# Flow turns of two attention stages: where mask tables are made, when finished chunks are copied out, and how next-turn projection work is spread

## The chip, the cores and the metric

One Trainium2 chip, one core. The program is one launch. The metric is device microseconds of that core, from three runs of the kernel before: 3243.58, 3242.65 and 3238.93, median 3242.65.

The engines are named as the profile names them: PE (TensorE), ACT (ScalarE), DVE (VectorE), POOL (GpSimd) and SP (SyncE, here only a DMA queue).

## The reference, cut to what matters

The model is two blocks in a row. The change touches two of their mixers. Each has 16 heads of width 64, over 1024 tokens. The first is forgetting attention (`fox` in the kernel):

```python
logits = einsum('bhtd,bhsd->bhts', qb, kb) * d ** -0.5 + F[:, :, q0:q1, None] - F[:, :, None, :q1]
probs  = softmax(where(mask_causal, logits, -inf)); out = probs @ vb      # F = cumsum(log_sigmoid(fz + fb))
y_f    = out * silu(fg)
```

The second is neighbourhood attention on a 16 x 64 grid with 256 context tokens (`nb` in the kernel):

```python
s   = einsum(q_r, k_reg) * d ** -0.5 + bias(rel_bias);  s = where(col_mask, s, NEG_INF)
p   = softmax(concatenate([s, q_r @ kc]));  o = p_lat @ v_reg + p_ctx @ vc
y   = (o * silu(g)) @ w_out
```

In both, q, k, v and g are projections of the same activations with a 1024-row weight matrix.

## The kernel before, in words

**Turns.** Both mixers are run by the class `Flow`. It works on two heads at a time, so each mixer has 8 turns (`PAIRS`). `plan` writes out by hand, before the program is built, one list of steps for each turn. PE, ACT and DVE each walk the same list and do their own part of each step, in its order, and wait on semaphores for each other. So the list is the order of each engine's queue.

**Fill.** The projections of float32 values are done as three matmuls (high x high, low x high, high x low). One chunk of a projection (512 tokens, or 256 for the context) takes 24 matmuls (`FULL`). Step `F n` issues the next n of them. Turn `it` fills with V and G of its own heads and with Q and K of the next turn's heads. That is 8 chunks in a fox turn (192 matmuls) and 10 in an nb turn (240). Chunks alternate between two PSUM banks, and step `E` copies a finished chunk out: for Q and K, ACT writes the high part and DVE then the low part. The first score of a turn (`head` in `pe`) waits for the last chunk of the turn before.

**Attention.** `S` is a score piece: PE multiplies, then DVE (line 1455) subtracts it from a mask table, writes it to SBUF and keeps the running minimum. There is one pair of score banks, so each `S` on PE waits until DVE has finished the one before. `X` is the exponential on ACT. A group `T` transposes up to four 128 x 128 blocks, ACT casts them to the high part, DVE subtracts for the low part (line 1466), and one group later `V` multiplies them with the values. There are two transpose banks, so `T` of group n waits until DVE has finished group n-2, counted over all groups. A fox turn has 20 groups in four segments, an nb turn has 26. The scores of segment s+1 are issued among the groups of segment s. `M`, `O`, `N` move, add and normalise a finished segment, `I` inverts its row sums.

**The end of a turn.** After the last group come the remaining `M`, `O`, `N` with 4 fill matmuls ahead of each, then `W` (ACT: silu of the gate), `Y` (DVE multiplies by the gate, line 1504; then ACT makes the high part, line 1416), the rest of the chunk, `D` (DVE subtracts for the low part, line 1509; ACT issues the two stores), and then the mask tables `B` for the next turn. A turn has two of these. In fox they are `nf_tri` for each head (line 1614). In nb they are `nb_bias` (line 2450) and `nb_mid` (line 2453), each for both heads. `L` is their load: ACT waits until all scores of the turn are shifted, then issues two DMAs. In the kernel before, `L` stands after the last group.

**Weights.** SP loads a 128 x 1024 unit of weights, and POOL splits it in two parts with two instructions (lines 210 and 212) as soon as PE has used up the unit that held the slot.

In fox the units' chunks are tokens 0 to 511, then 512 to 1023. The segments of query blocks go (4, 5), (6, 7), (2, 3), (0, 1).

Where the steps stand, counted in fill matmuls of a turn, in the kernel before. Fox: scores of the first segment at 6, 14, 23 and 31; groups from 57 to 144; last five `N`, `I`, `M`, `O`, `N` at 148 to 164; `D` and first table at 168; second table at 192. Nb: scores of the first segment at 6, 20, 35 and 49; groups from 81 to 168; last `N` at 180; `D` and first table at 192, second table at 216; end at 240.

Of the kernel before, what the change touches and what calls it, by code (L numbers as in the profile page):

```python
# [55 lines left out]
def build_program(nc, a):  # L56
# [9 lines left out]
    with ctx:  # L66
# [925 lines left out]
        class Flow:  # L992
# [109 lines left out]

            def plan(self, before, turns, final, tables, last_fill, side_by_side=False):

# [8 lines left out]
                def chunks_of(units, scores_before, side_by_side=False):  # L1113
                    new = []
                    parts = [(unit, i) for unit in units for i in range(len(unit[3]))]
                    if side_by_side:
                        parts.sort(key=lambda part: part[1] >= 2)
                    for (kind, it, unit, spans), i in parts:
                        c0, n = spans[i]
                        last, seq = i == len(spans) - 1, len(self.chunks)  # L1120
                        beside = side_by_side and seq < 4
                        b = (self.p_bank, self.p_bank + 1, self.o_bank, self.o_bank + 1)[seq] if beside \
                            else self.p_bank + seq % 2
                        count[final[kind]] += 1
                        count["chunk"] += not last
                        ch = {"kind": kind, "it": it, "unit": unit, "c0": c0, "n": n, "first": i == 0,
                              "last": last, "seq": seq, "scored": scores_before, "bank": b, "beside": beside,
                              "waits": self.user.get(b),
                              "done": (w_used, unit + 1) if last else (self.chunk, count["chunk"]),
                              "out": ({"act": self.act_out, "dve": self.dve_out}[final[kind]], count[final[kind]])}  # L1130
                        self.user[b] = ch["out"]
                        self.chunks.append(ch)
                        new.append(ch)
                    return new
# [9 lines left out]
                self.seg0 = count["seg"]  # L1144
                self.lead, l_turned = [], [0, 0]
                first = chunks_of(before, count["S"], side_by_side)
# [7 lines left out]
                for it, units in enumerate(turns):  # L1154
                    fill = chunks_of(units, count["S"] + n_scores)
                    steps, held = [], []
                    at = {"fill": 0, "S": 0}

                    scores, base_u = [], count["U"]
# [11 lines left out]
                    def fill_to(n):  # L1171
                        n = min(n, FULL * len(fill))
                        while at["fill"] < n:
# [3 lines left out]
                            if at["fill"] % FULL == 0:  # L1177
                                ch = fill[at["fill"] // FULL - 1]
                                if ch["kind"] in "QK" and at["S"] < n_scores:
                                    held.append(ch)  # L1180
                                else:
                                    steps.append(("E", ch))

                    def score(s):
                        s["l_free"] = l_turned[s["seg"] % 2]
                        steps.append(("S", s))
                        at["S"] += 1
                        if at["S"] == n_scores:
                            steps.extend(("E", ch) for ch in held)

# [7 lines left out]
                    lead = FULL * len(values)  # L1198
                    places = [(6 + (lead - 14) * i // len(scores[0]), "S", s) for i, s in enumerate(scores[0])]
                    places += [(FULL * (i + 1) + 9, "T", ch) for i, ch in enumerate(values)]  # L1200
# [11 lines left out]
                    n_groups = sum(len(g) for g in groups)  # L1212
                    start, main = at["fill"], FULL * sum(ch["kind"] in "VGQ" for ch in fill)
                    if final_turn:
                        n_groups = last_fill
                    todo, waiting, done = [], None, 0

                    def event():
# [5 lines left out]
                    for seg, rows in enumerate(groups):  # L1224
                        count["seg"] += 1
                        pending = list(scores[seg + 1]) if seg + 1 < len(scores) else []
                        for i, (items, adds) in enumerate(rows):
                            g = group("P", it, seg=seg, seg_n=count["seg"], items=items, adds=adds, starts=i == 0,
                                      ends=i == len(rows) - 1, exped=base_u + self.first_unit(seg + 1))
# [31 lines left out]
                    if final_turn:  # L1261
# [5 lines left out]
                        break  # L1267
                    steps.append(("L", it + 1, count["S"]))
                    while todo:
# [4 lines left out]
                    steps.append(("D", it, self.whole))  # L1274
                    for part in range(tables):
                        steps.append(("B", it + 1, part))
# [268 lines left out]
        def fox_units(it, kinds):  # L1545
            return [(kind, it, U_FOX + 4 * it + "QKVG".index(kind), [(0, CH), (CH, CH)]) for kind in kinds]

# [845 lines left out]
        def nb_units(it, kinds):  # L2393
# [5 lines left out]
                {"Q": "dve", "K": "dve", "V": "act", "G": "act"}, 2,  # L2399
                sum(len(nb.seg_groups(seg)) for seg in range(2)), True)  # L2400

# [299 lines left out]
```

## Time and profile before

| | |
|---|---|
| Median of three runs | 3242.65 us |
| Span of the profiled execution, first to last instruction | 3236.3 us |
| PE busy | 96% of the span |
| DVE busy | 62% |
| ACT busy | 40% |
| POOL busy | 23% |
| One fox turn (turns 1 to 6) | 77.03 us |
| One nb turn (turns 1 to 6) | 95.53 us |

The span is the time from the first to the last instruction of one execution. The 8 fox turns run from about 598 to 1215 us, the 8 nb turns from about 2363 to 3100 us. The last turn of each mixer has no next turn to fill with, and has its own layout. Matmul ends are modelled, so the idle time shown ahead of a matmul can be smaller than the time that was lost: start times are the safer reading.

### The profile page before, as it was taken

To read this page: it belongs to the slowest core of one execution; us is meant where nothing else is said; L and a number is where in the kernel's file an instruction comes from. 1 tells how busy PE (TensorE), PEld (TensorE's weight loads), DVE (VectorE), ACT (ScalarE), POOL (GpSimd) and SP (SyncE) were. 2 spreads that over 40 slices of the span, in tenths; PEclk is the share of its full clock that TensorE was granted. 3 is DMA by queue.
4 is the path that set the end of the run, shared out by engine and by line. 5 is a ranking of instruction groups with operands and counts; after the bars stand their busy time and mean duration, and the time that the engine had idled before them with its cause. 6 is when DMAs were issued, how large, how long until landed. Compare 5 with 4: busy or idle time off the path is not lost.

```text
span 3236.3 us, 47842 instructions
## 1 busy us (share of the span) xinstructions
PE 3109.7 (96%) x18134; PEld 2578.9 (80%) x18134; DVE 1999.7 (62%) x3834; ACT 1299.9 (40%) x2340; POOL 759.8 (23%) x324
## 2 busy tenths in 40 slices
PE   9999999999999989999899999999899999999987
PEld 6888888777777767877799889888677778777765
DVE  5676677555565657975755555556755555655555
ACT  5534443444444440022444444440344444454412
POOL 3223332322222213543211121113112112111221
PEclk9999999999999999999999999999999999999999
DMA  3111111111111137521200010153201111100141
GB/s 118 46 40 46 46 59 46 60 59 53 53 53 53 64 146 298 220 79 52 91 30 30 31 43 30 46 203 130 78 21 51 45 51 45 51 32 33 67 161 76
DMA packets 64828, 237.79 MB, mean 73 GB/s; under 512 B 7008, under 2 KB 10080, under 8 KB 63600
## 3 DMA queue, kind: packets, MB, share of 16 engines
q1 hardware_dynamic: 31680, 115.91, 9.9%
q10 hardware_dynamic: 32944, 119.10, 9.7%
q8 instruction: 135, 2.21, 0.3%
q14 instruction: 69, 0.57, 0.0%
HBM read 185.11 MB, written 49.87 MB: 73 GB/s over the span
## 4 chain that ended last, share of the span: by engine, by line
PE 79%; DVE 9%; ACT 5%; issue 2%; DVEq 2%; DMA 1%; ACTq 1%; SPq 0%
PE ps L1304 21%; PE ps L189 13%; PE ps L360 9%; PE ps L2223 7%; PE ps L1368 5%; PE ps L1334 4%; PE ps L1350 4%; PE ps L891 3%; PE ps L482 3%; PE ps L868 2%; PE ps L133 2%; DVE fox_l L1455 1%; PE ps L852 1%; DVE wa_l L941 1%; PE ps L853 1%
## 5 line engine op out<-in xcount | busy, mean ns | idle before, releaser
L210 POOL TENSOR_TENSOR w_hi<-raw,small 128x1024 fp32r<-128x1024 f32 x160 | 334.9, 2093 | 2393.7 <-PE ps L1304 1099.3
L212 POOL TENSOR_TENSOR w_lo<-raw,w_hi 128x1024 fp32r<-128x1024 f32 x160 | 424.8, 2655 | 22.8
L1304 PE MATMUL ps<-nb_u_hi,w_hi 128*128 128x512 f32 (+1 forms) x640 | 249.2, 389 | 6.1 <-DVE nb_q_lo L2470 4.2
L1304 PE MATMUL ps<-nb_u_hi,w_lo 128*128 128x512 f32 (+1 forms) x640 | 246.6, 385 | 0.0
L1304 PE MATMUL ps<-nb_u_lo,w_hi 128*128 128x512 f32 (+1 forms) x640 | 245.7, 384 | 0.0
L1466 DVE TENSOR_TENSOR nb_pt_lo<-ps,nb_pt_hi 128x512 fp32r<-128x512 f32 x208 | 143.9, 692 | 144.2 <-ACT nb_pt_hi L1393 143.9
L360 PE MATMUL ps<-u_hi,w_hi 128*128 128x512 f32 x528 | 212.8, 403 | 5.9 <-ACT silu_h L539 2.6
L1304 PE MATMUL ps<-u_hi,w_lo 128*128 128x512 f32 x512 | 208.9, 408 | 0.0
L360 PE MATMUL ps<-u_hi,w_lo 128*128 128x512 f32 x528 | 208.6, 395 | 0.0
L360 PE MATMUL ps<-u_lo,w_hi 128*128 128x512 f32 x528 | 208.4, 395 | 0.0
L1304 PE MATMUL ps<-u_hi,w_hi 128*128 128x512 f32 x512 | 208.3, 407 | 0.0
L1304 PE MATMUL ps<-u_lo,w_hi 128*128 128x512 f32 x512 | 207.5, 405 | 0.0
L1393 ACT CAST nb_pt_hi<-ps 128x512 fp32r<-128x512 f32 x208 | 122.1, 587 | 193.4 <-PE ps L1350 190.7
L1466 DVE TENSOR_TENSOR fox_pt_lo<-ps,fox_pt_hi 128x512 fp32r<-128x512 f32 (+1 forms) x160 | 102.0, 638 | 129.3 <-ACT fox_pt_hi L1393 128.8
L2223 PE MATMUL ps<-wa_u_hi,w_hi 128*128 128x512 f32 (+1 forms) x480 | 173.1, 361 | 4.3 <-DVE wa_u_lo L2156 1.9
L891 PE MATMUL ps<-wa_v,wa_pt 128*128 128x64 f32 x1344 | 176.5, 266 | 0.0
L2223 PE MATMUL ps<-wa_u_lo,w_hi 128*128 128x512 f32 (+1 forms) x480 | 171.1, 356 | 0.0
L2223 PE MATMUL ps<-wa_u_hi,w_lo 128*128 128x512 f32 (+1 forms) x480 | 171.0, 356 | 0.0
L902 ACT ACTIVATE wa_l<-wa_l,wa_nm 128x641 f32<-128x641 f32 (+2 forms) x160 | 119.3, 746 | 124.8 <-DVE wa_nm L941 123.6
L891 PEld LDWEIGHTS ps<-wa_v,wa_pt 128*128 128x128 f32 x1344 | 168.9, 192 | 0.0
L1393 ACT CAST fox_pt_hi<-ps 128x512 fp32r<-128x512 f32 (+1 forms) x160 | 87.0, 544 | 144.8 <-PE ps L1350 144.3
L1304 PEld LDWEIGHTS ps<-nb_u_hi,w_hi 128*128 128x128 f32 x640 | 121.6, 190 | 29.3 <-issue 11.6
(357 smaller groups left out, 8027.8 us busy)
## 6 DMA issues: line engine op xcount, KB each, us to landing
raw<-in_w_stream SPq DMA_DIRECT2D x160, 512.0 KB, 3.3
h_sb<-in_w_ada ACTq DMA_DIRECT2D x16, 1024.0 KB, 5.0
nf_b<-nf_rows ACTq DMA_DIRECT2D x16, 512.0 KB, 4.4
nb_bias<-in_rel_bias ACTq DMA_DIRECT2D x16, 448.0 KB, 3.8
y_parts<-wa_y_hi ACTq DMA_DIRECT2D x8, 640.0 KB, 3.0
y_parts<-wa_y_lo ACTq DMA_DIRECT2D x8, 640.0 KB, 4.2
la_out_yh<-y_parts SPq DMA_DIRECT2D x8, 640.0 KB, 10.0
la_out_yl<-y_parts SPq DMA_DIRECT2D x8, 640.0 KB, 11.1
```

The costliest lines, as they stand in the source:

```text
L189: mm = pe.matmul(out, w(slot, tiles[i]), u[:, first + i, cols], start=start and i == 0 and p == 0, stop=stop and i == len(tiles) - 1 and p ...
L210: pool.tensor_tensor(w_hi[:, s, :], raw[:, s, :], zero, ALU.add)
L212: pool.tensor_tensor(w_lo[:, s, :], raw[:, s, :], w_hi[:, s, :].bitcast(F32), ALU.subtract).then_inc(w_ready, 1)
L360: mm = pe.matmul(ps[:, b:b + CH], w(slot, k), u[:, k, ch["c"] * CH:(ch["c"] + 1) * CH], start=k == 0 and p == 0, stop=k == KT - 1 and p == 2)
L891: mm = pe.matmul(ps[:, o0:o0 + HD], self.pt[0:n, self.v_place[g] % 3, (c - c0) * P:(c - c0 + 1) * P], vals[0:n, vb, cols], start=c == 0, s ...
L1304: mm = pe.matmul(ps[:, b:b + ch["n"]], w(slot, k), u[:, k, ch["c0"]:ch["c0"] + ch["n"]], start=k == 0 and p == 0, stop=k == KT - 1 and p == 2)
L1334: mm = pe.matmul(ps[:, o:o + n], q[r, qc], k[r, key:key + n], start=p == 0, stop=p == 2)
L1350: mm = pe.transpose(out[:, j * P:(j + 1) * P], self.l_of(g["seg"], qi, hd)[:, l0:l0 + P], ident)
L1368: mm = pe.matmul(ps[:, o + o0:o + o0 + n], self.v[:, vb, kv if self.shared else hd, :], pt[:, g["high"] % 2, p0:p0 + n], start=g["starts"] ...
L1393: nc.scalar.copy(self.pt_hi[:, g["high"] % 2, 0:w], ps[:, t:t + w]).then_inc(self.high, 1)
L1466: dve.tensor_tensor(self.pt_lo[:, i, 0:w], ps[:, t:t + w], self.pt_hi[:, i, 0:w].bitcast(F32), ALU.subtract).then_inc(self.freed, 1)
L2223: mm = pe.matmul(ps[:, b * CH + t:b * CH + t + n], w(i % 2, k), u[:, k, t:t + n], start=k == 0 and p == 0, stop=k == KT - 1 and p == 2)
```

## The change

Five things in `Flow.plan`, and one in each mixer's call.

1. `pieces_until` counts, for each Q and K chunk, after how many score pieces of a turn its columns are no longer needed. A finished chunk is held back only for those, no longer for all scores.
2. In fox, the chunks of Q and K are made in the order tokens 512 to 1023, then 0 to 511.
3. `main`, the fill that is spread over the groups, has one K chunk more: 6 chunks become 7 in fox, 7 become 8 in nb. So 24 fill matmuls move from behind the last group to among the groups.
4. `L` is issued one group after the last score, and from three groups later one `B` is put ahead of each group. What isn't made there stays behind `D`.
5. The scores of the first segment are placed by their size, and in nb (`ahead_by` 1) the first piece of the second segment comes ahead of the groups as well.

In the last turn of a mixer 3 and 4 do nothing.

```diff
+            def pieces_until(self, kind, c0, n):
+                last, at = 0, 0
+                for blk in (blk for blocks in self.segments for blk in blocks):
+                    for piece in blk["pieces"]:
+                        at += 1
+                        spans = [(blk["b"] * P, P)] if kind == "Q" else [(key, w) for _, key, w in piece["runs"]]
+                        if any(a < c0 + n and c0 < a + w for a, w in spans):
+                            last = at
+                return last
...
+                        after = self.pieces_until(kind, c0, n) if kind in "QK" and self.turns is not None else 0
-                              "last": last, "seq": seq, "scored": scores_before, "bank": b, "beside": beside,
+                              "last": last, "seq": seq, "scored": scores_before + after, "after": after,
+                              "bank": b, "beside": beside,
...
-                    fill = chunks_of(units, count["S"] + n_scores)
+                    fill = chunks_of(units, count["S"])
+                    all_scored = count["S"] + n_scores
...
-                                if ch["kind"] in "QK" and at["S"] < n_scores:
+                                if at["S"] < ch["after"] or held:
                                     held.append(ch)
...
-                        if at["S"] == n_scores:
-                            steps.extend(("E", ch) for ch in held)
+                        while held and held[0]["after"] <= at["S"]:
+                            steps.append(("E", held.pop(0)))
...
-                    places = [(6 + (lead - 14) * i // len(scores[0]), "S", s) for i, s in enumerate(scores[0])]
+                    ahead = scores[0] + scores[1][:ahead_by]
+                    sizes = [sum(n for _, _, n in s["blk"]["pieces"][s["piece"]]["runs"]) + 3 * P // 2 for s in ahead]
+                    places = [(6 + (lead - 14) * sum(sizes[:i]) // sum(sizes), "S", s) for i, s in enumerate(ahead)]
...
-                    start, main = at["fill"], FULL * sum(ch["kind"] in "VGQ" for ch in fill)
+                    first_k = [ch for ch in fill if ch["kind"] == "K"][:1]
+                    start, main = at["fill"], FULL * (sum(ch["kind"] in "VGQ" for ch in fill) + len(first_k))
...
+                    since, made = -1 if final_turn else 0, 0
...
+                            since += since > 0 or since == 0 and at["S"] == n_scores
+                            if since == 1:
+                                steps.append(("L", it + 1, all_scored))
+                            if since > 3 and made < tables:
+                                steps.append(("B", it + 1, made))
+                                made += 1
...
-                    steps.append(("L", it + 1, count["S"]))
...
-                    for part in range(tables):
+                    for part in range(made, tables):
...
         def fox_units(it, kinds):
-            return [(kind, it, U_FOX + 4 * it + "QKVG".index(kind), [(0, CH), (CH, CH)]) for kind in kinds]
+            return [(kind, it, U_FOX + 4 * it + "QKVG".index(kind), [(CH, CH), (0, CH)] if kind in "QK"
+                     else [(0, CH), (CH, CH)]) for kind in kinds]
...
-                sum(len(nb.seg_groups(seg)) for seg in range(2)), True)
+                sum(len(nb.seg_groups(seg)) for seg in range(2)), True, 1)
```

## Rows read from the trace of the kernel before

**Rows 1.** The page, first part: busy time of each engine, its share and instructions.
```profile
PE 3109.7 (96%) x18134; PEld 2578.9 (80%) x18134; DVE 1999.7 (62%) x3834; ACT 1299.9 (40%) x2340; POOL 759.8 (23%) x324
```
**Rows 2.** Windows, a fox and an nb turn: length, busy (instructions), PE clock, DMA.
```profile
745.27:822.30 77.03, 75.32 (x434) 59.21 (x433) 45.91 (x122) 35.86 (x74) 17.95 (x9) 1.00 0.15 55
2523.33:2618.86 95.53, 93.53 (x595) 75.19 (x595) 54.28 (x125) 44.87 (x83) 17.15 (x9) 1.00 0.12 43
```
**Rows 3.** PE's waits in that fox turn: total us, times, longest.
```profile
PE ps L1334 <- DVE fox_nm L1455: 0.9, 3, 0.4
PE ps L1350 <- DVE fox_pt_lo L1466: 0.6, 1, 0.6
```
**Rows 4.** PE's waits in that nb turn, same columns.
```profile
PE ps L1350 <- ACT nb_l L1384: 1.4, 2, 0.8
PE ps L1334 <- DVE nb_nm L1455: 0.5, 1, 0.5
```
**Rows 5.** Timeline of PE at a fox turn's end: start, length, line, out<-in [idle before].
```profile
748.80 0.38 PE L1355 MATMUL ps<-consts,fox_ri_rows 128*128 128x128 f32 x2
...
749.70 0.39 PE L1304 MATMUL ps<-u_hi,w_lo 128*128 128x512 f32 x1
...
756.57 0.40 PE L1304 MATMUL ps<-u_hi,w_lo 128*128 128x512 f32 x1
757.08 0.50 PE L1334 MATMUL ps<-fox_k_hi,fox_q_hi 64*128 64x512 f32 x2
...
760.38 0.33 PE L1334 MATMUL ps<-fox_k_hi,fox_q_hi 64*128 64x128 f32 x2 [0.29 <-DVE fox_nm L1455]
```
**Rows 6.** Timeline of ACT and DVE at the same place.
```profile
752.01 0.58 ACT L1581 CAST fox_k_hi<-ps 128x512 fp32r<-128x512 f32 x1
749.80 1.23 DVE L1504 TENSOR_TENSOR fox_y<-fox_y,fox_silu 128x1024 f32<-128x1024 f32 x1
752.62 0.69 DVE L1606 TENSOR_TENSOR fox_k_lo<-ps,fox_k_hi 128x512 fp32r<-128x512 f32 x1 [1.60 <-ACT fox_k_hi L1581]
753.23 1.22 DVE L1509 TENSOR_TENSOR fox_y<-fox_y,fox_y_hi 128x1024 f32<-128x1024 f32 x1
...
756.85 1.86 DVE L1614 TENSOR_TENSOR nf_tri<-nf_b,consts 128x1024 f32<-128x1024 f32 x1
758.89 0.75 DVE L1455 CUSTOM_DVE_ANT_0 fox_l<-ps,nf_b,fox_top 128x512 f32<-128x512 f32 x1 [0.18 <-issue]
```
**Rows 7.** Timeline of POOL: both splits of one unit in fox, second split in nb.
```profile
755.74 1.89 POOL L210 TENSOR_TENSOR w_hi<-raw,small 128x1024 fp32r<-128x1024 f32 x1 [7.54 <-PE ps L1304]
757.77 3.19 POOL L212 TENSOR_TENSOR w_lo<-raw,w_hi 128x1024 fp32r<-128x1024 f32 x1
...
2524.33 2.41 POOL L212 TENSOR_TENSOR w_lo<-raw,w_hi 128x1024 fp32r<-128x1024 f32 x1
```
**Rows 8.** Timeline of DVE in an nb turn: both tables, a group's low part, an addition.
```profile
2531.55 2.09 DVE L2450 TENSOR_TENSOR nb_bias<-nb_bias,consts 128x896 f32<-128x896 f32 x2
...
2535.88 1.55 DVE L2453 TENSOR_TENSOR nb_mid<-nb_bias,consts 128x640 f32<-128x640 f32 x2
...
2606.41 0.69 DVE L1466 TENSOR_TENSOR nb_pt_lo<-ps,nb_pt_hi 128x512 fp32r<-128x512 f32 x1 [0.22 <-ACT nb_pt_hi L1393]
...
2608.63 0.41 DVE L1494 TENSOR_TENSOR nb_y<-ps,nb_o_other 64x256 f32<-64x256 f32 x1
```
**Rows 9.** Timeline of PE in nb: first and fourth group of the last segment.
```profile
2605.13 0.63 PE L1350 MATMUL ps<-consts,nb_l 128*128 128x128 f32 x4 [0.63 <-ACT nb_l L1384]
...
2610.62 0.55 PE L1350 MATMUL ps<-consts,nb_l 128*128 128x128 f32 x3
```
**Rows 10.** PE after a long wait elsewhere (timeline), and two windows of 7 and 15 us.
```profile
2341.85 0.55 PE L1304 MATMUL ps<-nb_u_hi,w_hi 128*128 128x256 f32 x1 [4.17 <-DVE nb_q_lo L2470]
1410.00:1425.00 15.00, 11.66 (x49) 8.67 (x48) 11.87 (x7) 2.95 (x3) 6.41 (x3) 1.00 0.38 140
2341.00:2348.00 7.00, 6.15 (x33) 5.62 (x34) 2.92 (x6) 0.37 (x1) 1.49 (x1) 0.76 0.23 75
```

More of the change, by code:

```diff
@@ L1101, in seg_groups, with plan @@
                 return groups
-            def plan(self, before, turns, final, tables, last_fill, side_by_side=False):
+            def pieces_until(self, kind, c0, n):
[7 more added lines that the diff above has]
+                return last
+            def plan(self, before, turns, final, tables, last_fill, side_by_side=False, ahead_by=0):
                 self.chunks = []
@@ L1144, in plan @@
                 self.seg0 = count["seg"]
-                self.lead, l_turned = [], [0, 0]
+                self.lead, l_turned, self.turns = [], [0, 0], None
                 first = chunks_of(before, count["S"], side_by_side)
@@ L1225, in plan @@
                         count["seg"] += 1
-                        pending = list(scores[seg + 1]) if seg + 1 < len(scores) else []
+                        pending = [s for s in scores[seg + 1] if s not in ahead] if seg + 1 < len(scores) else []
                         for i, (items, adds) in enumerate(rows):
+                            since += since > 0 or since == 0 and at["S"] == n_scores
[4 more added lines that the diff above has]
+                                made += 1
                             g = group("P", it, seg=seg, seg_n=count["seg"], items=items, adds=adds, starts=i == 0,
```

## The prediction

> **What bounds the kernel.** I read the busy line first: PE works 96% of the span, DVE 62% [rows 1]. So the time is PE's queue plus its waits. The change adds and removes no matmul. Then I cut out one steady turn of each mixer. In fox PE is busy 75.3 of 77.03 us, in nb 93.5 of 95.53 us [rows 2]. Turns 0 to 6 of each mixer get the change in full, so 7 + 7 turns share some 26 us of shown idle time. That is most of what can be won. PE's waits in the turn say where it sits. In fox: three times for the shift of the score before, once for the low part of a group [rows 3]. In nb: twice for exponentials, once for a shift [rows 4]. All but one lie among the groups and the first scores. One fox wait (0.29 us) is at the second score of the turn, behind the mask table [rows 5, 6]. Where DVE and ACT have to answer PE quickly, a few tenths are lost; behind the groups, with plain fill, nothing is. That plain fill is what the change spends.
>
> **Among the groups: the gain.** 24 fill matmuls more lie among 20 fox groups and 26 nb groups. A fill matmul takes 0.229 us (749.70 to 756.57 is 30 of them) [rows 5]. So each fox group gets 1.2 x 0.229 = 0.27 us more cover, each nb group 0.9 x 0.229 = 0.21 us. Without the 0.29 at the head, fox has about 1.2 us of shown idle there [rows 3, 5]. Each such wait also hides some 0.15 us ahead of it (756.57 to 757.08 shows no idle, yet is 0.28 us more than a fill step [rows 5]). The wait between two scores with 4 fills between them gets a fifth fill and keeps about 0.2, the wait for a low part keeps 0.2, the others go. Gain 1.4 us for a fox turn (bounds 0.8 and 1.8). In nb the piece put ahead removes the wait for a shift (0.5), and brings the exponentials of segment 2 a group forward, which removes the first wait for them (0.8) [rows 4]. The second stays, since `L`, with its wait for the last shift and two DMA issues, is now ahead of those exponentials in ACT's queue. With 0.3 hidden the gain is 1.6 us (bounds 1.0 and 2.2). Holding a chunk less long is worth nothing by itself: in the list of before no chunk is held for more than 2 fills. Placing by size is worth nothing on PE in fox beyond the second score, counted below. The two last turns win from it and the piece ahead: 1.5 us together (0 to 3).
>
> **The end of a fox turn: first cost.** `main` now ends at 168, so the same five steps stand at 172 to 188, `W` and `Y` at 188, and the last K chunk ends at 192 with `E` right behind `Y` in ACT's queue. In the kernel before, the first K chunk had this very place: `N` at 748.80, chunk finished at 749.70, but its copy started at 752.01 and its low part at 752.62, as ACT first had to serve `Y` [rows 5, 6]. There nobody waited for it. Now it is the chunk that the next turn's first score waits for, and only 6 fills lie between. PE would be ready at 749.70 + 7 x 0.229 = 751.3. From the start of the low part to the score it is 0.83 us (756.25, which is 757.08 less 0.83; the 0.69 of the instruction and the semaphore), so the score starts at 752.62 + 0.83 = 753.45. It waits 2.15 us, against 0.28 now (757.08 less 756.80) [rows 5]. Cost 1.87 us (bounds 1.2 and 2.3).
>
> **Second cost: `D` and a table ahead of the first shift.** With the last score in group 16 of 20, the counter reaches 4 only at group 20. So one `nf_tri` table is made there (1.2 us, hidden: that group has 2 blocks and DVE half a period free). The other stays behind `D`. DVE's queue is then k_lo, `D`, table, shift. POOL's split of the next unit starts when the K unit is used up, 0.54 us behind its last matmul, so at 750.24 in this picture. What DVE and POOL do to each other is in rows 6 and 7: the table issued at 756.85 lasts 1.86 us, not 1.22, and ends 1.08 us after POOL's first split does (757.63). The second split, issued at 757.77, lasts 3.19 us, not 2.41. Each waited for the other's whole instruction. With `Y` at 749.80 to 751.03 POOL's first split gets through from 750.89, the second follows 2.03 us later (755.74 to 757.77) at 752.93, and ends at 755.33. `D`, ready at 753.23, waits for that, the table follows 1.15 us later, ends at 757.70, the shift starts 0.18 us later at 757.88. In the kernel before the next score came 1.49 us behind the shift's start (758.89 to 760.38), so now at 759.37. PE, with 11 fills where there were 8, would be ready at 753.45 + (3.30 - 0.29) + 3 x 0.229 = 757.15 [rows 5]. It waits 2.22 us against 0.29. Cost 1.93 us; without the collision `D` and the table take 2.35 us from 753.23, the score comes at 757.25, and the cost is -0.19. I take the collision, as the split is issued three microseconds before `D`.
>
> The Trainium skill, page SBUF — State Buffer, section "Who interferes with whom", says that a vector instruction with two SBUF inputs and a GpSimd instruction that reads SBUF exclude each other for the whole instruction. The rows show that for the table alone; for `Y` and `D` (two SBUF inputs too) no row has an overlap. Were `D` free of it, only the table would wait, and the score would come at 755.33 + 1.22 + 0.18 + 1.49 = 758.2, 1.2 us earlier a turn.
>
> Fox: 7 x (1.87 + 1.93 - 1.4) = **+16.8 us**.
>
> **Nb: tables among the groups.** All scores are issued at group 17, so the tables stand ahead of groups 21 and 22, the second and third of the last segment. The Q chunk's `E` falls at fill 168, in group 21 too, and `O` of segment 3. Before, the tables lay behind `D`, where DVE had time. Count from the start of group 20's `T` (2605.13) [rows 9]. Its low part starts at +1.28 (2606.41), the next DVE instruction 0.61 later at +1.89 [rows 8]. Then the first table, 2.09, to +3.98; 0.18 for the drain; low part of group 21 at 4.16; q_lo at 4.77; `O` at 5.38, two of 0.43 [rows 8], to 6.24. Now the second table, 1.55, then 0.18, and the low part of group 22. Group 23's `T`, behind `N` in the same two banks, needs it. POOL splits from the end of the Q unit: issued at about 3.1, it waits for the first table, starts at 3.84, its second split at 5.87 to 8.28 (2.41 [rows 7]). The second table would want to start at 6.24, so it waits to 8.28 and ends at 9.83. The low part starts at 10.0, and `T` 0.83 later at 10.85. PE would be ready at +5.8: 2610.62 less 2605.13 is 5.49, two fills more, less the little it waited [rows 9]. It waits **5.05 us**. If the second table slips in ahead of the split it is 8.8 and the wait 3.0 us. The margin is 0.4 us, so the collision is likelier. The tables leave the tail of the turn, but there they were hidden, so nothing comes back. Nb: 7 x (5.05 - 1.6) = **+24.2 us**.
>
> **Sum.** 16.8 + 24.2 - 1.5 = +39.5 us, on a span of 3236.3, which stands 6.3 us below the median of the runs: 3275.8 of span, 3282 as a run.
>
> **Rivals.**
> - **No collision with POOL** (the vector engine's instructions follow each other closely enough to keep POOL out, or fall beside it). Fox 7 x (1.87 - 0.19 - 1.4) = 2.0, nb 7 x (3.0 - 1.6) = 9.8, less 1.5: +10.3, **3253**. For it: the margins are 0.3 to 0.4 us. Against: two places must both escape.
> - **The tables are covered** (other side). Place: nb groups 21 to 23. If DVE has caught up when the tables come, because PE's slack of two groups is larger than I count, the waits of 5.05 us don't appear. It decides where that wait falls under the 1.6 us gained. Then fox +0.3 a turn, nb -1.6: 2.0 - 11.2 - 1.5 = -10.7, **3232**; with the fox K chunk in time as well, 3220. For it: DVE is busy only 54 of 95 us in a turn [rows 2]. Against: 2.09 + 0.69 + 0.69 + 0.86 + 1.55 + 0.69 us of DVE work lie in two groups of about 1.9 us.
> - **PE's clock falls as well.** After 4.17 us of waiting the granted clock is 0.76 over 7 us, so 0.24 x 7 = 1.7 us are lost; with 3.3 us idle in pieces over 15 us it stays 1.00 [rows 10]. In each nb turn that is 7 x 1.7 = 12 us more, **3294**. I leave it out, as PE comes out of 60 us of full work here, and keep it in the range. The Trainium skill, page TensorE: Matmul & The Clock Gate, section "Why this matters for your kernels", warns of long idle gaps between bursts; it would side with this rival.
> - **It does little**: fox and nb gains meet smaller costs, **3243**.
>
> **How the numbers follow.** Forecast 0.47 (own range 3266 to 3291), no collision 0.25, clock 0.10, covered 0.12, little 0.06. The range takes all but the covered case and some edges: 3244 to 3299. A measurement of this kernel can tell about 0.2% (6.5 us) from no change. Slower by more than that: 0.47 + 0.10 + 0.21 of the no-collision case = 0.78. Same: 0.10. Faster: 0.12.
>
> **What would show it.** In the trace after: the fox score at fill 6 waits about 2 us for fox_k_lo, the next one about 2 us for fox_nm; one nf_tri table lies in the last group; `D` or the table lasts 2 to 3 us beside a split. In nb the `T` of group 23 waits some 5 us for nb_pt_lo, and an nb_mid table lasts over 2 us. The waits of rows 3 and 4 shrink. Fox turns last 79.4, nb turns 99.0 us. Wrong if the first score finds its K chunk ready, or if nb turns get shorter.

## The result, and the profile after

The changed kernel takes 3302.7 us (median of 4 runs, 3295.7 to 3306.7) against 3241.8 us for the kernel before (also of 4): ratio 1.0186, interval 1.0171 to 1.0200. It is slower, as forecast, but by 61 us and not by 39.5: the time lies 3.7 us above the top of the range. The profiled execution took 3300.42 us with a span of 3298.6.

The page's busy line, and PE's waits in the whole run (total us, times, longest) from the view of waits:

```profile
PE 3130.2 (95%) x18134; PEld 2597.0 (79%) x18134; DVE 2010.7 (61%) x3834; ACT 1303.4 (40%) x2340; POOL 764.1 (23%) x324
```
```profile
PE ps L1373 <- DVE nb_pt_lo L1489: 30.1, 8, 4.2
PE ps L1357 <- DVE fox_k_lo L1630: 13.8, 7, 2.0
PE ps L1357 <- DVE fox_nm L1478: 13.3, 17, 2.1
PE ps L1327 <- DVE nb_q_lo L2494: 5.9, 1, 5.9
```

The instruction counts are those of before, but PE is busy 20.5 us longer with them [rows 1]. The mean granted clock fell from 0.988 to 0.979 of full speed. The three largest waits that are new or larger are the three that the prediction named. The one that the kernel before had most of (for exponentials in nb, 12.1 us) fell to 4.1.

**Where it lies.** The fox stage ends 23.1 us later, the nb stage with the first matmuls of the projection behind it is 37.3 us longer, the stages between add 2.0: 62.3 us of span. The seven nb turns between first scores last 100.6 us in the mean (99.97 to 101.18), where they lasted 95.5 (the first nb score of the kernel before stands at 2347.66 us, not at the 2363 given for the start of the nb turns); six fox turns last 80.1 (79.29 to 80.80), where they lasted 77.03. As windows, in the columns of [rows 2]: a fox turn that kept the clock, two that didn't, and two nb turns in a row.

```profile
681.17:760.46 79.29, 75.09 (x432) 59.26 (x433) 45.19 (x123) 36.50 (x74) 17.75 (x9) 1.00 0.16 54
760.46:840.51 80.05, 76.62 (x432) 60.36 (x433) 45.01 (x123) 36.51 (x74) 17.73 (x9) 0.98 0.16 53
1082.42:1161.73 79.31, 76.64 (x432) 60.21 (x433) 45.16 (x123) 36.50 (x74) 17.74 (x9) 0.98 0.15 54
2474.90:2574.87 99.97, 94.86 (x595) 76.56 (x595) 56.53 (x124) 44.95 (x83) 17.93 (x9) 0.98 0.12 42
2574.87:2675.99 101.12, 96.00 (x594) 77.43 (x595) 56.52 (x124) 44.95 (x83) 17.94 (x9) 0.97 0.11 41
```

**The head of a fox turn**, timelines of PE, DVE and POOL (start, length, line, out<-in, idle before), to be read against [rows 5 to 7]:

```profile
840.51 0.49 PE L1357 MATMUL ps<-fox_k_hi,fox_q_hi 64*128 64x512 f32 x2 [1.98 <-DVE fox_k_lo L1630]
846.24 0.33 PE L1357 MATMUL ps<-fox_k_hi,fox_q_hi 64*128 64x128 f32 x2 [2.04 <-DVE fox_nm L1478]
```
```profile
759.62 0.69 DVE L1630 TENSOR_TENSOR fox_k_lo<-ps,fox_k_hi 128x512 fp32r<-128x512 f32 x1 [1.60 <-ACT fox_k_hi L1605]
760.23 3.14 DVE L1532 TENSOR_TENSOR fox_y<-fox_y,fox_y_hi 128x1024 f32<-128x1024 f32 x1
763.30 1.21 DVE L1638 TENSOR_TENSOR nf_tri<-nf_b,consts 128x1024 f32<-128x1024 f32 x1
764.69 0.75 DVE L1478 CUSTOM_DVE_ANT_0 fox_l<-ps,nf_b,fox_top 128x512 f32<-128x512 f32 x1 [0.18 <-issue]
```
```profile
757.26 2.52 POOL L210 TENSOR_TENSOR w_hi<-raw,small 128x1024 fp32r<-128x1024 f32 x1 [11.31 <-PE ps L1327]
759.92 2.37 POOL L212 TENSOR_TENSOR w_lo<-raw,w_hi 128x1024 fp32r<-128x1024 f32 x1
```

The first score waits for `k_lo`. `D` is issued at 760.23, 0.31 us after POOL's second split began, and ends 1.1 us after that split's end (762.29): 3.14 us for an instruction of 1.22 [rows 6]. The table and the shift follow in DVE's queue, and the second score waits for the shift.

**The last segment in nb**, PE and DVE, to be read against [rows 8, 9]:

```profile
2443.14 0.63 PE L1373 MATMUL ps<-consts,nb_l 128*128 128x128 f32 x4 [0.41 <-ACT nb_l L1407]
2453.58 1.11 PE L1373 MATMUL ps<-consts,nb_l 128*128 128x128 f32 x4 [4.23 <-DVE nb_pt_lo L1489]
```
```profile
2445.03 2.08 DVE L2474 TENSOR_TENSOR nb_bias<-nb_bias,consts 128x896 f32<-128x896 f32 x2
...
2449.27 3.49 DVE L2477 TENSOR_TENSOR nb_mid<-nb_bias,consts 128x640 f32<-128x640 f32 x2
```
```profile
2446.15 2.71 POOL L210 TENSOR_TENSOR w_hi<-raw,small 128x1024 fp32r<-128x1024 f32 x1 [22.26 <-PE ps L1327]
2449.00 2.34 POOL L212 TENSOR_TENSOR w_lo<-raw,w_hi 128x1024 fp32r<-128x1024 f32 x1
```

`T` of group 23 starts 10.44 us behind `T` of group 20. The two halves of the mid table take 3.49 us beside the split, not 1.55; the low part that `T` waits for starts behind them, at 2452.84. What the prediction left out stands in PE's rows right behind the wait, and in the clock column (the last but two) of the windows around it:

```profile
2456.63 0.63 PE L1327 MATMUL ps<-nb_u_hi,w_hi 128*128 128x512 f32 x1
2457.06 0.63 PE L1327 MATMUL ps<-nb_u_lo,w_hi 128*128 128x512 f32 x1
```
```profile
2448.00:2453.00 5.00, 1.35 (x8) 0.93 (x8) 4.88 (x6) 0.08 (x1) 3.20 (x2) 0.85 0.09 27
2453.00:2457.00 4.00, 3.42 (x12) 3.08 (x13) 2.02 (x5) 0.58 (x1) 0.00 (x0) 0.50 0.27 101
2457.00:2461.00 4.00, 4.00 (x24) 3.42 (x23) 0.71 (x2) 1.17 (x2) 0.00 (x0) 0.84 0.00 0
2461.00:2465.00 4.00, 4.00 (x28) 3.48 (x27) 1.90 (x3) 1.47 (x3) 0.00 (x0) 1.00 0.00 0
```

Fill matmuls step by 0.43 us (2456.63 to 2457.06), not by 0.229: the granted clock is at its lower level, 1.2 of 2.4 GHz. It is back some 5 us after `T` (0.84 over the 4 us from 2457 is 1.3 us at the lower level).

### The profile page after: what moved, and what is told of

Its sections match the earlier page's. It is cut to its first block, busy times and chain, and to the rows that moved or that the text cites. A ratio compares the mean times of both kernels' runs of the same rounds, so it can differ in the third digit from the quotient of the medians.

```text
span 3298.6 us, 47842 instructions
## 1 busy us (share of the span) xinstructions
PE 3130.2 (95%) x18134; PEld 2597.0 (79%) x18134; DVE 2010.7 (61%) x3834; ACT 1303.4 (40%) x2340; POOL 764.1 (23%) x324
## 4 chain that ended last, share of the span: by engine, by line
PE 77%; DVE 11%; ACT 5%; DVEq 2%; issue 2%; DMA 2%; ACTq 1%; SPq 0%
PE ps L1327 20%; PE ps L189 13%; PE ps L360 9%; PE ps L2247 7%; PE ps L1391 5%; PE ps L1357 5%; PE ps L1373 4%; PE ps L891 3%; PE ps L482 3%; PE ps L868 2%; PE ps L133 2%; PE ps L852 1%; DVE nb_pt_lo L1489 1%; PE ps L853 1%; DVE wa_l L941 1%
## 5 line engine op out<-in xcount | busy, mean ns | idle before, releaser
L210 POOL TENSOR_TENSOR w_hi<-raw,small 128x1024 fp32r<-128x1024 f32 x160 | 344.6, 2154 | 2451.8 <-PE ps L1327 1153.9
L212 POOL TENSOR_TENSOR w_lo<-raw,w_hi 128x1024 fp32r<-128x1024 f32 x160 | 419.4, 2621 | 22.8
L1373 PE MATMUL ps<-consts,nb_l 128*128 128x128 f32 x832 | 130.2, 280 | 34.2 <-DVE nb_pt_lo L1489 30.1
L1373 PEld LDWEIGHTS ps<-consts,nb_l 128*128 128x128 f32 x832 | 105.4, 145 | 64.4 <-DVE nb_pt_lo L1489 40.4
```

Source lines behind the costliest of these rows:

```text
L210: pool.tensor_tensor(w_hi[:, s, :], raw[:, s, :], zero, ALU.add)
L212: pool.tensor_tensor(w_lo[:, s, :], raw[:, s, :], w_hi[:, s, :].bitcast(F32), ALU.subtract).then_inc(w_ready, 1)
L1373: mm = pe.transpose(out[:, j * P:(j + 1) * P], self.l_of(g["seg"], qi, hd)[:, l0:l0 + P], ident)
```

## The experiments

The first eight of these kernels add parameters to `plan`; the edits show the core. The theory after the result: the waits named in the prediction make two thirds of the loss, and the clock that falls behind them most of the rest.

**Fox's K chunk back behind the groups.** Nb is left as changed.

```diff
-                    first_k = [ch for ch in fill if ch["kind"] == "K"][:1]
+                    first_k = [ch for ch in fill if ch["kind"] == "K"][:spread_k]     # fox 0, nb 1
```

> The changed kernel, but in fox the K chunk stays behind the last group, as before (fill over the groups ends at 144); the rest of the change stays. Theory (the K chunk that the next turn's first score needs comes out of the copy engine too late, and one table stands ahead of the first shift): both waits of some 2 us at the start of a fox turn go, the first back to 0.1 to 0.3 us, the second to under 0.3, fox turns go from 80.1 to about 76.8 us, the granted clock in them is 1.00 again; nb turns stay at 100.5. Time about 3302.7 - 7 x 3.3 - 2 = 3278. Rival (the fox loss comes from the load and table among the groups): fox turns stay near 79 to 80 and the time near 3300.

Measured: 3279.5 us, ratio 1.0119 (1.0103 to 1.0136), span 3277.8. Fox turns fall back to 77.0 us, the waits for `fox_k_lo` are gone, and nb stays at 30.1 us of waits for `nb_pt_lo`. So both waits at the head of a fox turn need the spread K chunk, and it costs 20.8 us of span. The load and one table still stand among the groups there.

**Nb tables three groups later** (ahead of groups 24 and 25, not 21 and 22). Fox is left as changed.

```diff
-                            if since > 3 and made < tables:
+                            if since > tables_from and made < tables:     # fox 3, nb 6
```

> The changed kernel, but in nb the two tables stand ahead of groups 24 and 25 instead of 21 and 22, so neither beside the Q chunk's copy nor beside POOL's split of the next unit. Theory (the nb wait is DVE's queue of table, low part, q_lo, additions, table, with 2 us of it spent on POOL's split): the wait of PE for nb_pt_lo falls from 4.2 us to about 1.3, no nb_mid pair lasts over 1.6 us, the clock in nb turns is 1.00, nb turns go from 100.5 to about 95.2; time about 3302.7 - 37 = 3265. Rival (any table among the groups costs its full 3.6 us of DVE time): the wait is 3 us or more and nb turns last over 97 us, time over 3278.

Measured: 3259.5 us, 5.5 below the expected 3265, ratio 1.0055 (1.0039 to 1.0072), span 3257.7. Nb turns last 95.05 us, 5.6 less than in the changed kernel and 0.5 less than before. DVE's timeline of it, whole pairs of tables:

```profile
2448.96 2.09 DVE L2476 TENSOR_TENSOR nb_bias<-nb_bias,consts 128x896 f32<-128x896 f32 x2
2451.12 0.69 DVE L1491 TENSOR_TENSOR nb_pt_lo<-ps,nb_pt_hi 128x512 fp32r<-128x512 f32 x1
2451.73 1.55 DVE L2479 TENSOR_TENSOR nb_mid<-nb_bias,consts 128x640 f32<-128x640 f32 x2
```

Both tables now lie behind `O`, `q_lo` and POOL's splits, and cost PE almost nothing. It is where the tables stand that costs, not that they stand among groups.

**All tables back behind `D`**, and their load behind the last group, with the spread K chunks kept.

```diff
-                            if since > 3 and made < tables:
+                            if since > tables_from and made < tables:     # 99 for both
```

> The changed kernel, but load and both tables of both mixers stand behind the last group, as before; the K chunk, the order of the chunks, the piece put ahead and the placing by size stay. Theory: nb loses its long wait and keeps the gain, nb turns about 94.0 us at a clock of 1.00 (95.53 before); in fox the first score still waits 2 us for fox_k_lo, and now two tables stand ahead of the first shift, so the second wait is about 3.3 us, fox turns about 81. Time about 3241.8 + 28 + 2 - 11 = 3261. Rival (the extra fill among the groups brings nothing): nb turns stay at 95.5 and the time is about 3272.

Measured: 3292.4 us, ratio 1.0159 (1.0142 to 1.0176), span 3290.7. The expectation was 31 us too low: it had the fox waits right (2.0 and 3.3 us) and this wait, new in nb, not at all. That wait, and DVE's timeline at the end of an nb turn:

```profile
PE ps L1359 <- DVE nb_k_lo L2500: 18.5, 7, 2.6
```
```profile
2479.76 3.78 DVE L2476 TENSOR_TENSOR nb_bias<-nb_bias,consts 128x896 f32<-128x896 f32 x2
2483.62 0.42 DVE L2500 TENSOR_TENSOR nb_k_lo<-ps,nb_k_hi 128x256 fp32r<-128x256 f32 x1
```

I had taken the tail of an nb turn to hide the tables as before. With a K chunk gone from it, 24 fills less, the low part of the last K chunk stands behind a table that POOL holds (3.78 us, not 2.09), and the next turn's first score waits for it. The prediction says of nb's tail "there they were hidden, so nothing comes back": true of the kernel before only. The changed kernel needs its early tables because it spreads the chunk.

**Only the nb tables and their load moved** (no piece ahead, no spread chunk, fox as before). One thing differs from the text of the expectation: the first scores are still placed by size and chunks held by what uses them, in both mixers, so that its fox turns last 76.65 us and not 77.03.

> The kernel before (fox with its own order, no K chunk moved in either mixer, no piece put ahead) with one part of the change: in nb the load comes one group after the last score and the two tables stand ahead of groups 21 and 22. There neither the Q chunk's end nor POOL's split falls among these groups. Theory: DVE's work between two low parts is then 5.3 us, PE waits about 2.7 us for nb_pt_lo, against 4.6 (by start times) with the split and q_lo; nb turns 98.2 us, 99 if the clock falls as well. Time 3241.8 + 19 to 26, about 3262. Rival (the tables cost nothing without the K chunk): nb turns 95.5, time 3242.

Measured: 3263.1 us, ratio 1.0062 (1.0045 to 1.0079), span 3261.1; nb turns last 98.3 to 99.9 us. Its waits for `nb_pt_lo` are 12.4 us at transposes and 9.4 at values. Over the kernel before this is 25 us of span, and nb turns are 3.3 us longer in the mean, of the 5.1 of the changed kernel. So most of nb's loss needs neither the spread chunk nor the piece ahead.

**Only the placing**: scores placed by size, chunks held by what uses them, one nb piece ahead; tables and K chunks as before.

> The kernel before with one part of the change alone: the first scores placed by size in both mixers, and in nb the first piece of the second segment put ahead of the groups. No K chunk moved, load and tables behind the last group, fox chunks in their old order. Theory (the gain is real but small: in fox the wait at the second score goes, in nb one wait for a shift and one for exponentials): fox turns 76.6 us (77.03 before), nb turns 94.2 (95.53), time 3242 - 3 - 9 = 3230. Rival (PE's waits only move to the next place): turns within 0.3 us of before, time 3240 or more.

Measured: 3229.0 us, ratio 0.9954 (0.9940 to 0.9968), span 3224.8. This is the part of the change that pays, and the fastest version of this study with the whole computation. A fox and an nb turn of it:

```profile
757.43:834.07 76.64, 75.23 (x432) 59.27 (x433) 45.82 (x123) 36.24 (x75) 17.96 (x9) 1.00 0.16 55
2534.85:2629.38 94.53, 93.36 (x596) 75.24 (x596) 54.44 (x124) 44.86 (x83) 17.17 (x9) 1.00 0.13 44
```

0.4 us a fox turn and 1.0 us an nb turn are won [rows 2], 9.8 of the 11.5 us of span. Against it the fox turns with the K chunk back (77.0) and the nb turns with late tables (95.05) are 0.4 and 0.5 us longer. So with its long waits gone in one mixer, the rest of the change still brings nothing over the placing. The two repairs together were not run.

**PE kept busy in nb's long wait.** The changed kernel with 18 matmuls more in each of the seven turns, whose results are not used, just ahead of `T` of group 23. They fit in the wait.

```diff
+                            if since == 6 and keep_busy:
+                                steps.append(("Z", all_scored, keep_busy))
```

> The changed kernel, with 18 matmuls more in each nb turn that compute nothing that is used: they write the free score banks at the place where PE waits for nb_pt_lo of group 22. They take 18 x 0.229 = 4.1 us of a wait of 4.6. Theory (the wait makes the granted clock fall to the lower level for some 4.6 us behind it, which costs about 1.9 us a turn): the clock in nb turns is 1.00, the matmuls behind that place last as long as elsewhere, nb turns go from 100.5 to 98.6, time 3302.7 - 13 = 3290. Rival (the clock costs nothing, as DVE sets the pace behind the wait): nb turns stay at 100.5, time 3303.

Measured: 3288.4 us, ratio 1.0138 (1.0123 to 1.0154), span 3285.0: 126 matmuls more, and 13.6 us of span less. PE at that place, and a whole turn:

```profile
2451.28 4.24 PE L1390 MATMUL ps<-nb_u_hi 128*128 128x512 f32 x18
2455.72 0.66 PE L1378 MATMUL ps<-consts,nb_l 128*128 128x128 f32 x4 [0.20 <-DVE nb_pt_lo L1499]
```
```profile
2474.88:2573.58 98.70, 97.63 (x613) 78.73 (x614) 56.57 (x124) 44.99 (x83) 17.98 (x9) 1.00 0.12 42
```

The `T` starts 10.50 us behind that of group 20 (2445.22), so the wait for DVE is as long as before. Only the clock differs. In the changed kernel nb turns alternate between 0.98 and 0.97, with 100.0 and 101.1 us; here all have 1.00 and last 98.7. The fall behind the wait costs 1.3 and 2.4 us by turns, 1.9 in the mean.

**Fox's last K chunk ahead of the gate.** `Y` stands behind the chunk's copies, so that `k_lo` is early.

```diff
-                    steps += [("W", it), ("Y", it, self.whole)]
                     fill_to(FULL * (at["fill"] // FULL + 1))
+                    steps.append(("Y", it, self.whole))
```

> The changed kernel, but at the end of a fox turn the last K chunk's fill and copy stand ahead of Y (gate multiply and its high part) instead of behind it. Theory: ACT then copies the chunk as soon as it is made, and the wait for fox_k_lo at the first score falls from 2.0 us to 0.3 or less. But Y, D and the table now all stand between that chunk and the first shift in DVE's queue, and each waits for POOL: the wait at the second score grows from 2.0 to about 4.3 us, and fox turns stay near 80 us, time 3303 within 8. Rival (the queue in ACT is the whole cost at a turn's end): fox turns fall to about 78.2 and the time to 3289.

Measured: 3314.0 us, ratio 1.0209 (1.0193 to 1.0224), span 3315.2. The wait for `k_lo` is gone, and the next score takes over all of it:

```profile
769.61 0.47 PE L1363 MATMUL ps<-fox_k_hi,fox_q_hi 64*128 64x128 f32 x2 [4.09 <-DVE fox_nm L1484]
```

```profile
761.77 1.68 DVE L1533 TENSOR_TENSOR fox_y<-fox_y,fox_silu 128x1024 f32<-128x1024 f32 x1
764.58 2.23 DVE L1538 TENSOR_TENSOR fox_y<-fox_y,fox_y_hi 128x1024 f32<-128x1024 f32 x1 [1.12 <-ACT fox_y_hi L1445]
```
```profile
760.48 1.89 POOL L210 TENSOR_TENSOR w_hi<-raw,small 128x1024 fp32r<-128x1024 f32 x1 [11.31 <-PE ps L1333]
762.52 3.20 POOL L212 TENSOR_TENSOR w_lo<-raw,w_hi 128x1024 fp32r<-128x1024 f32 x1
```

`Y`, `D` and the table now lie ahead of the shift in one piece. `Y` and `D` each end 1.1 us behind the split that they met (762.37 and 765.72), and the second split, 3.20 us, waits for `Y`. Two waits of 2.0 us became one of 4.1, and the clock of the turn is 0.96. The time is 11 us above the expected 3303, 3 us outside what was allowed for; the wait came out near the expected 4.3, but the lower clock was not in the expectation. The order at the turn's end moves the cost; DVE's work between the last group and the first shift is what must shrink.

**One early nb table, ahead of group 25, the other behind `D`**, on the version with only the placing; the K chunk and the load in nb stand among the groups as in the changed kernel.

```diff
-                            if since > 3 and made < tables:
+                            if since > 7 and made < tables and (since - 8) % 2 == 0:
```

> Like the placing alone, but nb has its K chunk among the groups, the load one group after the last score, one table ahead of group 25 and the other behind D. Theory: with one table of 2.1 us far from the Q chunk and POOL's split DVE keeps up, no wait for nb_pt_lo over 0.5 us, clock 1.00; the extra fill takes the rest of the small waits, and nb turns are 93.9 to 94.3, time about 3229. Rival (the extra fill brings nothing over the placing): nb turns as in the placing alone or longer, time at or above that kernel's.

Measured: 3251.9 us, ratio 1.0025 (1.0015 to 1.0035), span 3250.3, 23 us above the expected 3229. The mid table, left in the tail, falls beside a split and ahead of the last `k_lo` (2445.76):

```profile
2442.44 3.25 DVE L2478 TENSOR_TENSOR nb_mid<-nb_bias,consts 128x640 f32<-128x640 f32 x2
```

The first score then waits for it seven times, 14.7 us in all. It is the same collision as in the run with the tables back, with one table.

**POOL's second split cut short**, in the changed kernel and in the one before. From the third unit on, POOL's second instruction writes 128 of its 1024 columns. This takes the collision away and leaves the lists of steps as they are.

```diff
             pool.tensor_tensor(w_lo[:, s, 0:n], raw[:, s, 0:n], w_hi[:, s, 0:n].bitcast(F32),     # n = 128
                                ALU.subtract).then_inc(w_ready, 1)
```

> The changed kernel with one thing left out everywhere but in the first two units: GpSimd's second splitting operation (w_lo) writes 128 of its 1024 columns, so that it should take about 0.3 us instead of 2.4 to 2.8; the low weights that the projections use are then stale. Theory (GpSimd's splits hold VectorE's operations with two SBUF inputs): in the fox turns D, 3.14 us of VectorE beside that operation, falls to its 1.22 and the wait of the first scores for the shift from 2.0 us to about 0.1; in nb the mid table, 3.49 us beside it, falls to about 1.6 and the longest wait for pt_lo from 4.2 us to about 2.3. Fourteen times 1.9 us is 27 us, and the clock that no longer falls as deep gives another 5 to 10: 3268 us, 3262 to 3277. The wait for k_lo (2.0 us, seven times) stays. Rival (VectorE's own queue alone makes the waits, the split has nothing to do with them): both waits keep their lengths, 3303 us, less what the kernel before gains from the same cut.

> The kernel before with the same part left out (GpSimd's second splitting operation at 128 of 1024 columns in all units but the first two), as the measure for the other run. The trace of before has few places where PE waits behind such a collision: 3234 us, 3228 to 3243. By the theory the change then costs 34 us of its 61 (3268 over 3234); by the rival it still costs about 60.

Measured: changed kernel 3250.0 us, ratio to the kernel before 1.0019 (1.0010 to 1.0029), span 3243.1; kernel before with the same cut 3222.9 us, ratio 0.9935 (0.9918 to 0.9952), span 3220.7. With the cut the change costs 27 us of time (22 of span), not 61. Waits, and DVE and POOL, in the changed kernel with the cut:

```profile
PE ps L1373 <- DVE nb_pt_lo L1489: 16.9, 8, 2.4
PE ps L1357 <- DVE fox_k_lo L1630: 13.8, 7, 2.0
...
PE ps L1357 <- DVE fox_nm L1478: 3.9, 10, 1.2
```
```profile
831.80 1.23 DVE L1532 TENSOR_TENSOR fox_y<-fox_y,fox_y_hi 128x1024 f32<-128x1024 f32 x1
...
2418.24 1.60 DVE L2477 TENSOR_TENSOR nb_mid<-nb_bias,consts 128x640 f32<-128x640 f32 x2
```
```profile
831.49 0.46 POOL L212 TENSOR_TENSOR w_lo<-raw,w_hi 128x128 fp32r<-128x128 f32 x1
```

`D` takes 1.23 us, not 3.14, the mid table 1.60, not 3.49; the wait for the shift all but goes, the wait for `nb_pt_lo` falls from 4.2 to 2.4, and the wait for `k_lo`, which no split touches, stays. The rival (DVE's queue alone) is out. The expectation for the changed kernel was 18 us too high, and that for the kernel before 11: other stages gain from the short split too (last section), and the clock's part was a guess.

## Why the prediction was right or wrong

**Right in place and nearly in size: the waits.** `k_lo` was forecast at 2.15 us of wait and shows 1.98. The shift was forecast at 2.22 and shows 2.04, with `D` behind POOL's second split. The `T` of group 23 was forecast 10.85 us behind that of group 20 and stands at 10.44; its wait, counted from the +5.8 at which PE would be ready, is 4.6 us and not 5.05. In the turn whose clock stayed at 1.00 fox lasts 79.29 us, forecast 79.4. With PE kept busy nb lasts 98.7, forecast 99.0. So the forecast's sum of waits and gains holds where the clock does and nothing else comes in.

**The choice of the collision was right.** The rival without it is the pair of kernels with the short split. It gave 96.9 us (95.53 and 1.4) for nb; the turn of that run that kept its clock lasts 96.8, and its `T` stands at +8.56 where the rival had +8.8.

**`D` beside a split.** The prediction's rows had the exclusion for the table alone, and it priced the case that `D` is free of it. The rows now show it for `D` (3.14 us against 1.23) and, in the run with the chunk ahead of the gate, for `Y` (1.68 against 1.23), as the Trainium skill says on its page SBUF — State Buffer, section "Who interferes with whom".

**Wrong: "PE's clock falls as well ... I leave it out, as PE comes out of 60 us of full work here".** This is the failed step: the sum has nothing for the clock. PE had full work until 2449, and after 4.2 us of waiting its clock was 0.50 over the next 4 us. What it did long before did not save it. The rival priced this at 1.7 us an nb turn, 12 us, 3294; the run with PE kept busy gives 1.9 a turn and 13.6 us of span. [rows 10] had shown the fall once, with nearly the right price. I argued the exception from a difference (the work ahead) that no row tied to the clock. The page TensorE: Matmul & The Clock Gate of the Trainium skill, section "Why this matters for your kernels", warns of long idle gaps between bursts, and the trace agrees for gaps of 4 us.

The other row of [rows 10], 11.66 us of work in 15 at a clock of 1.00, was no support either. The changed kernel has the same stretch with the same busy time, and there the clock falls right behind it. Waits of 1.5 and 1.7 us in that stretch are followed by the lower clock in one trace and not in the other:

```profile
1433.00:1448.00 15.00, 11.66 (x49) 8.65 (x48) 11.87 (x7) 3.04 (x3) 6.57 (x3) 1.00 0.40 140
1448.00:1452.00 4.00, 4.00 (x12) 3.14 (x11) 0.23 (x1) 1.28 (x1) 0.00 (x0) 0.58 0.00 0
```

**Left out altogether in fox: the clock, and the load's place in ACT's queue.** The mean turn is 0.7 us above the forecast of 79.4. The turns differ by two things.

- *Where the lower clock falls.* In the turns from 840 and 1001 us, and in the last one, it lies behind the second wait: the fourth score comes 12.7 us behind the first, not 11.2. The first two of these turns last 80.8. In the turns from 760, 921 and 1082 it lies between the first score and the second, and costs nothing: the second score stands at +5.72 as in the turn at 1.00, and only its wait shrinks, from 2.0 to 0.45 us, as the shift on DVE sets the time. The turn from 1082 has a clock of 0.98 and still lasts 79.31, against 79.29 at 1.00.
- *The load.* `L` has two DMA issues in ACT's queue, now ahead of the high part of a group. They take 0.81 us in the turn from 681, but 1.64 and 1.90 in those from 760 and 921. There the high part comes late, and PE waits 0.79 and 1.06 us for `fox_pt_lo`, which makes 80.05 and 80.36 of 79.3. The first turn loses 0.6 us so. The prediction weighed `L` in ACT's queue for nb only. Why some issues take longer was not followed up.

```profile
741.95 0.81 ACTq L1581 DMA_DIRECT2D nf_b<-nf_rows  x2
...
821.18 1.64 ACTq L1581 DMA_DIRECT2D nf_b<-nf_rows  x2
822.86 0.59 ACT L1416 CAST fox_pt_hi<-ps 128x512 fp32r<-128x512 f32 x1 [1.56 <-PE ps L1378]
```

What decides which turns get how much of the lower clock stays open.

**The rest of the miss.** Span is 22.8 us above the forecast of 3275.8. Seven nb turns at 1.6 over 99.0 are 11.4. The fox stage is 23.1 longer where 16.8 less its share of the last turns' gain, 0.75, was forecast: 7.1, nearly all of it the clock (three times 1.5) and the load (0.6, 0.8 and 1.1). The stages between are 2.0 longer: 75 matmuls of line 189 there take 19.04 us, not 17.45, at a lower clock. That leaves 2.3, in nb. From its start to the first score it takes 1.1 us more, behind the wait for `nb_q_lo`, where the lower clock lasts longer. That this wait is shown as 5.9 us where it was 4.2 [rows 10] costs nothing: the matmul behind it starts 25.1 us later than before (2366.95), and the stage itself starts 25.3 later. The last nb turn is 1.4 us shorter (81.67, not 83.07), so the gain forecast for the last turns is there, and the stage behind it is 1.5 longer.

**Half right: "what is moved was hidden, so nothing comes back".** It is right for the forecast, as the tables' old place was free. But it treats the tables and the spread chunk as separate edits. Put back behind `D` with the chunk spread, the tables cost 2.6 us of wait in each nb turn.

**The gain among the groups** was put at 1.4 us (fox) and 1.6 (nb) a turn. It can't be read alone, since it comes with the spread chunk. The placing alone gives 0.4 and 1.0. The turns at full clock tell more: 79.29 less 77.03 is 2.26, and the two waits less the 0.28 and 0.29 us that stood there before are 3.45, which leaves a gain of 1.2 for fox. For nb the wait of 4.6 less the 3.2 by which the turn at full clock is longer leaves 1.4. So in both mixers the waits and the gains were put too large by 0.2 to 0.5 us, and these errors cancel in part: that the turns at full clock come within 0.3 us of the forecast is partly luck.

**The range.** It ended at 3299, 5 us above the rival with the clock, as if nothing could stand on top of that case. Forecast bounds of the waits (1.2 to 2.3) and the clock are not alternatives: the longer wait brings the clock down more often. With the wait of 2.4 us in the run with the short split three of seven nb turns kept 1.00, with 4.2 us none did. The forecast's own range reached 3291; with the clock's 12 us on top of that, the top would have been 3303.

## What to carry to other kernels

A wait of several microseconds on PE must be priced twice: its length, and the slow matmuls behind it (here 1.9 us for each wait of 4.2, although PE had full work before). If another engine sets the time of what follows, the slow matmuls can cost nothing. When work is moved from a place where it was hidden, write down for the new place which queue it joins, who stands behind it, and which engine's instructions hold it up at that time: here the same two tables cost 5.6 us a turn or nothing, by three groups. Fill matmuls at the end of a turn are cover for the next turn's first operands; taking them away needs the work behind them to become shorter first.

## What the runs showed of the hardware beyond that

**DVE and POOL hold each other up in other stages too.** In the kernel before, an addition with two SBUF inputs (`la_acc`, 128x1280) takes 3524 ns in the mean of seven; with POOL's second split cut short it takes 1579. From the views of groups by line, the kernel before first:

```profile
L2096 DVE TENSOR_TENSOR la_acc<-la_acc,la_h 128x1280 f32<-128x1280 f32 x7 | 24.7, 3524 | 0.6
```
```profile
L2096 DVE TENSOR_TENSOR la_acc<-la_acc,la_h 128x1280 f32<-128x1280 f32 x7 | 11.1, 1579 | 0.6
```

These are 13.6 us of DVE time, and the kernel before as a whole gains 15.6 us of span by the short split. How much of the 15.6 comes from these additions was not shown.

**The lower clock outlasts the wait.** It was 0.85 over the 5 us that hold the wait, 0.50 over the next 4, 0.84 over the next 4, then 1.00, with PE busy 3.4 to 4.0 of each 4 us. In fox, with its two waits within 6 us, the lower clock came behind the first in one turn (0.73 over 760 to 764) and behind the second in the next (0.67 over 848 to 852).
